# Splitting 32 of the 42 input projections of the second block into three f32r products each

## The reference, cut to what matters

```python
def second_block(x, norm_mix, w_in, sinks, lam_re, ...):
    h = rms_norm(x, norm_mix[l])
    qa, ka, va, u, qm, km, vm, gates = split_in(h @ w_in[l])
    oa = swa_attention(qa, ka, va, sinks[l], slopes_swa)
    ya = oa @ w_o_swa[l]
    ys = s5_ssm(u, ...)
    z = jax.nn.gelu(ys).astype(x.dtype) @ w_glu[l]
    yb = (z[..., :SSM_WIDTH] * jax.nn.sigmoid(z[..., SSM_WIDTH:])) @ w_o_ssm[l]
    om = moba_attention(qm, km, vm, slopes_moba)
    yc = om @ w_o_moba[l]
    g = jax.nn.sigmoid(gates)
    mixed = (g[..., :D_MODEL] * ya + g[..., D_MODEL:2 * D_MODEL] * yb
             + g[..., 2 * D_MODEL:] * yc)
    x = x + mixed @ w_out[l]
```

## Time and profile before

| | us |
|---|---|
| median of 3 runs | 2204.14 |
| lowest and highest | 2203.28, 2205.13 |
| the profiled execution, its own time | 2205.18 |
| its span in the trace | 2203.4 |
| PE busy, share of the span | 2121.9, 96% |
| DVE busy | 853.8, 39% |
| ACT busy | 543.4, 25% |
| POOL busy | 89.9, 4% |

### The profile page before, as it was taken

One profiled execution on the slowest core, in us unless ns is written; L12 is line 12 of the kernel. 1 busy time (PEld: TensorE's weight loads), 2 busy tenths in 40 slices (PEclk: granted clock), 3 DMA queues, 4 the chain that ended last, 5 costly groups with the idle time before them and its releaser, 6 DMA issues.

```text
span 2203.4 us, 35696 instructions
## 1 busy us (share of the span) xinstructions
PE 2121.9 (96%) x15114; PEld 1312.8 (60%) x15114; DVE 853.8 (39%) x1576; ACT 543.4 (25%) x1013; POOL 89.9 (4%) x109
## 2 busy tenths in 40 slices
PE   6999999999999999998889999999999999999998
PEld 2666688888864673433323343334433877889998
DVE  4798523334532432032001210110022467666765
ACT  4124322224431421011000100000011134444443
POOL 0000000000000000000000000000501200001300
PEclk9999999999999999999989999999999999999999
DMA  9885232323211549999999999999995332344451
GB/s 387 333 354 191 77 115 77 114 76 105 82 39 47 207 184 379 355 376 402 417 413 408 389 402 378 407 401 418 413 405 212 127 115 77 115 152 174 173 189 57
DMA packets 160740, 536.71 MB, mean 244 GB/s; under 512 B 7120, under 2 KB 31824, under 8 KB 139728
## 3 DMA queue, kind: packets, MB, share of 16 engines
q1 hardware_dynamic: 160448, 534.08, 63.4%
q0 software_dynamic: 144, 0.52, 0.1%
HBM read 533.53 MB, written 1.05 MB: 243 GB/s over the span
## 4 chain that ended last, share of the span: by engine, by line
PE 84%; DVE 6%; DMA 5%; DVEq 3%; issue 1%; ACT 1%; SPq 0%; ACTq 0%
PE psum L1422 15%; PE psum L968 11%; PE psum L975 10%; PE psum L976 10%; PE psum L977 10%; PE psum L1426 7%; PE psum L1447 7%; PE psum L1451 3%; DMA X<-in_o_exp_w 2%; DVE region L2344 2%; DVEq L2347 1%; PE psum L992 1%; DMA region<-in_o_exp_w 1%; PE psum L1349 1%; DMA ring<-in_o_exp_w 1%
## 5 line engine op out<-in xcount | busy, mean ns | idle before, releaser
L975 PE MATMUL psum<-region_r 128*128 128x512 f32 (+1 forms) x1360 | 468.2, 344 | 14.2 <-DVE region L2356 3.2
L976 PE MATMUL psum<-region_r 128*128 128x512 f32 (+1 forms) x1264 | 425.4, 337 | 0.0
L977 PE MATMUL psum<-region_r 128*128 128x512 f32 (+1 forms) x1136 | 388.0, 342 | 0.0
L975 PEld LDWEIGHTS psum<-region_r 128*128 128x128 f32 x1360 | 258.7, 190 | 59.6 <-issue 20.3
L976 PEld LDWEIGHTS psum<-region_r 128*128 128x128 f32 x1264 | 240.7, 190 | 24.6
L977 PEld LDWEIGHTS psum<-region_r 128*128 128x128 f32 x1136 | 215.5, 190 | 24.8
L1422 PE MATMUL psum<-ring,region 128*32 128x512 f32 (+1 forms) x2064 | 203.8, 527 | 0.8 <-DMA ring<-in_o_exp_w 0.8
L1422 PEld LDWEIGHTS psum<-ring,region 128*32 128x32 f32 x2064 | 65.9, 111 | 118.4 <-issue 102.7
L968 PE MATMUL psum<-H,ring 128*128 128x256 f32 x576 | 128.7, 380 | 0.0
L968 PEld LDWEIGHTS psum<-H,ring 128*128 128x128 f32 x576 | 108.3, 190 | 16.5 <-ACT region L2059 1.3
L1983 ACT ACTIVATE region<-psum 128x256 f32<-128x256 f32 (+2 forms) x56 | 24.8, 450 | 376.2 <-PE psum L1373 278.0
(11 more groups left out here) (399 smaller groups left out, 2679.2 us busy)
## 6 DMA issues: line engine op xcount, KB each, us to landing
ring<-in_o_exp_w SPq DMA_DIRECT2D x151, 1024.0 KB, 12.4
region<-in_o_exp_w SPq DMA_DIRECT2D x118, 1024.0 KB, 14.2
ring<-in_w_ada SPq DMA_DIRECT2D x24, 2048.0 KB, 10.1
H<-in_o_exp_w SPq DMA_DIRECT2D x46, 1024.0 KB, 15.0
ring<-in_w_ff SPq DMA_DIRECT2D x16, 2048.0 KB, 7.9
ring<-in_e_ffn_w SPq DMA_DIRECT2D x22, 1024.0 KB, 7.9
X<-in_o_exp_w SPq DMA_DIRECT2D x21, 1024.0 KB, 14.5
ring<-in_w_in SPq DMA_DIRECT2D x10, 2048.0 KB, 8.0
```

What stands on the lines that cost most here:

```text
L975: pe.matmul(out, a_hi, b_hi, start=first, stop=False)
L976: pe.matmul(out, a_hi, b_lo, start=False, stop=False)
L977: mm = pe.matmul(out, a_lo, b_hi, start=False, stop=last)
```

## The change

- The chunks are taken in the order A, QM, QA, B, gates. The ten items of A and QM stay whole and come first (`WHOLE` = 10 instead of nine). The 32 items of QA, B and the gates are of a new kind, "split", and fill the eight rounds with four each.
- A split item is `product` over eight tiles: 24 f32r products of 128x256 instead of eight float32 products.
- ACT rounds the weights of a split item (`proj_high`): two instructions of 128x512, or one of 128x1024, depending on the buffer. There are three such buffers, used in turn (the last four items use two). Three items are rounded ahead, before ACT copies `bb_T`; each later one right after the `take` of the item that had its buffer, which is mostly the one three before.
- POOL subtracts (`L3109`), from the ring's weights to the same place, in pieces of the same sizes: 21 or 22 items with two pieces of 128x512 and ten with one of 128x1024.
- The normed input is split once: ACT rounds it between the first eight `take`s, and DVE subtracts in place (eight instructions of 128x256) when the last whole item is done.
- The counts of the semaphores that this shares with other stages are raised to fit.

The diff, cut to its core:

```diff
-C2_A, C2_B, C2_QA, C2_QM, C2_GATE, C2_SWA, C2_GLU, C2_MOBA, C2_SSM, C2_OUT, C2_FF1, C2_FF2 = (
+C2_A, C2_QM, C2_QA, C2_B, C2_GATE, C2_SWA, C2_GLU, C2_MOBA, C2_SSM, C2_OUT, C2_FF1, C2_FF2 = (
     0, 1, 2, 3, 4, 10, 11, 12, 13, 14, 16, 24)
...
+        + [(C2_QA, "split", 128 * i, ("qa", i)) for i in range(4)]
+        + [(C2_B, "split", 0, ("u", 2)), (C2_B, "split", 128, ("u", 3)),
+           (C2_B, "split", 256, ("qm", 0)), (C2_B, "split", 384, ("qm", 1))]
+        + [(C2_GATE + i // 4, "split", 128 * (i % 4), ("gate", i)) for i in range(24)])
+WHOLE = sum(p[1] != "split" for p in PROJ)
+PROJ_UNITS = len(PROJ) - WHOLE
+UNIT_OF = [i % 3 for i in range(PROJ_UNITS - 4)] + [1, 0, 1, 0]
+UNITS_BEFORE = Z_GROUPS + PROJ_UNITS
+UNITS_AFTER = [[i for i in range(3, PROJ_UNITS) if max(j for j in range(i) if UNIT_OF[j] == UNIT_OF[i]) == after]
+               for after in range(PROJ_UNITS)]
...
+        proj_hi = reg_r(25600, KT, T)
+        proj_parts = [[(range(0, 4), rstd_r[:, 0, :]), (range(4, KT), rstd_r[:, 1, :])],
+                      [(range(0, 4), reg_r(16896, 512)), (range(4, KT), reg_r(27648, 512))],
+                      [(range(0, KT), reg_r(5120, 1024))]]
...
+                elif kind == "split":
+                    if t == WHOLE:
+                        pe.wait_ge(s_n_lo_ready, KT)
+                    pe.wait_ge(s_weights_lo, Z_GROUPS + t - WHOLE + 1)
+                    mm = product(b[:, 0:T], [(hi[:, k - ks[0], :], proj_unit(t, [k], ring_r)[:, 0, :], proj_hi[:, k, :], H_lo[:, 0, k, :])
+                                             for ks, hi in proj_pieces(t) for k in ks], True, True)
...
-            for t in CHUNK_ITEMS[C2_A] + CHUNK_ITEMS[C2_B]:
+            for t in range(WHOLE):
                 project(t)
...
+            def proj_high(t):
+                n = PROJ[t][0]
+                if t in (items[0] for items in CHUNK_ITEMS):
+                    act.wait_ge(w_in[n % RING], landed2(n))
+                for ks, hi in proj_pieces(t):
+                    a = act.activation(hi, proj_unit(t, ks), ACT.Copy)
+                a.then_inc(s_weights_hi, 1)
...
                 a.then_inc(s_proj_sb, 1)
+                if t >= WHOLE:
+                    for ahead in UNITS_AFTER[t - WHOLE]:
+                        proj_high(WHOLE + ahead)
...
+            for t in range(WHOLE):
                 take(t)
+                if t < KT:
+                    act.wait_ge(s_h_ready, h_before(N_MIX2) + t + 1)
+                    act.activation(proj_hi[:, t, :], H[:, 0, t, :], ACT.Copy).then_inc(s_tile_hi, 1)
+            act.wait_ge(s_diag_ready, 1)
+            for i in range(3):
+                proj_high(WHOLE + i)
...
+            dve.wait_ge(s_proj_ready, WHOLE)
+            for k in range(KT):
+                dve.wait_ge(s_tile_hi, 2 * KT + k + 1)
+                dve.tensor_tensor(H_lo[:, 0, k, :], H[:, 0, k, :], proj_hi[:, k, :].bitcast(F32), ALU.subtract).then_inc(s_n_lo_ready, 1)
...
+            for t in range(WHOLE, len(PROJ)):
+                pool.wait_ge(s_weights_hi, Z_GROUPS + t - WHOLE + 1)
+                for ks, hi in proj_pieces(t):
+                    x = pool.tensor_tensor(proj_unit(t, ks, ring_r), proj_unit(t, ks), hi.bitcast(F32), ALU.subtract)
+                x.then_inc(s_weights_lo, 1)
```

More of the change, by code:

```diff
@@ L249 @@
 BRANCH_UNITS = 4 * len(BRANCHES)
-UNITS_BEFORE, VALUES_BEFORE = Z_GROUPS, 4
+VALUES_BEFORE = 4
 B_SPLIT = 4
@@ L361 @@
 PROJ = ([(C2_A, "dup", 0, ("ka", 0)), (C2_A, "dup", 64, ("ka", 1)), (C2_A, "tok", 128, ("va", 0)),
-         (C2_A, "feat", 256, ("u", 0)), (C2_A, "feat", 384, ("u", 1)),
-         (C2_B, "feat", 0, ("u", 2)), (C2_B, "feat", 128, ("u", 3)),
-         (C2_B, "feat", 256, ("qm", 0)), (C2_B, "feat", 384, ("qm", 1))]
-        + [(C2_QA, "feat", 128 * i, ("qa", i)) for i in range(4)]
+         (C2_A, "feat", 256, ("u", 0)), (C2_A, "feat", 384, ("u", 1))]
         + [(C2_QM, "feat", 128 * i, ("qm", 2 + i)) for i in range(2)]
         + [(C2_QM, "dup", 256, ("km", 0)), (C2_QM, "dup", 320, ("km", 1)), (C2_QM, "tok", 384, ("vm", 0))]
-        + [(C2_GATE + i // 4, "feat", 128 * (i % 4), ("gate", i)) for i in range(24)])
+        + [(C2_QA, "split", 128 * i, ("qa", i)) for i in range(4)]
[8 more added lines that the diff above has]
+               for after in range(PROJ_UNITS)]
 CHUNK_ITEMS = [[t for t, p in enumerate(PROJ) if p[0] == c] for c in range(C2_SWA)]
@@ L572, in build @@
         gain = sb("gain", P, 4, KT, 2)
-        rstd = sb("rstd", P, 2, 512)
+        with nc.sbuf_tensor("rstd", [P, 2, 512], F32) as rstd:
+            pass
+        rstd_r = sb("rstd_r", P, 2, 512, dt=F32R)
         warm = sb("warm", P, 1)
@@ L784, in branch_hi, with proj_unit, proj_pieces @@
             return unit_hi[u % B_SPLIT].rearrange("p (k h c) -> p k h c", k=4, h=2)
+        proj_hi = reg_r(25600, KT, T)
+        proj_parts = [[(range(0, 4), rstd_r[:, 0, :]), (range(4, KT), rstd_r[:, 1, :])],
+                      [(range(0, 4), reg_r(16896, 512)), (range(4, KT), reg_r(27648, 512))],
+                      [(range(0, KT), reg_r(5120, 1024))]]
+        def proj_unit(t, ks, memory=ring):
+            n, _, c, _ = PROJ[t]
+            return memory[:, n % RING, :].rearrange("p (k n) -> p k n", k=KT)[:, ks[0]:ks[-1] + 1, c:c + P]
+        def proj_pieces(t):
+            return [(ks, v.rearrange("p (k n) -> p k n", n=P)) for ks, v in proj_parts[UNIT_OF[t - WHOLE]]]
         def cols(w, c, n, rows=None):
```

6 lines of the change are left out of this document (3 added, 3 removed).

## The result

The changed kernel takes 2252.8 us (median of 4 runs, 2250.8 to 2256.5) against 2204.6 for the kernel before beside it: 1.022 times as long, with a 95% interval of 1.0202 to 1.0237. The forecast was 2241 in a range of 2212 to 2264. The profiled execution of the changed kernel is its longest one (2256.5, span 2254.7); set against the profile of before (2203.4) it is 51.3 longer, 3 more than the medians say.

The account below looks back on a forecast made before the run. The prediction took PE and DVE as balanced, with DVE's chain bounding the rounds up to the first `turn2`. Its terms, -0.5 + 0.6 + 14 + 18 + 6 = +38, less 1 for rounding, on 2204.1 gave 2241 us, range 2212 to 2264.

Parts of the forecast that it names:

- Making PE faster there gains nothing: In the rounds, from the drive to the first `turn2`, the chain needs DVE alone for 12.4 us; PE's items fit beside.
- Rival 1: In the rounds PE is the bound after all and POOL's work hides, so the gain arrives: 2191 us; chance 5%.
- Rivals 2 and 3: DVE and POOL collide only in slack (2204 to 2208, 8%), or only in elementwise instructions, not scans (2219, 15%).
- Rival 4: In the rounds POOL becomes the bound at 4 us an item, giving rounds of 28: 2265 to 2300; chance 10%.
- Ahead of the rounds: Before round 0: one more whole item, +3.5, and ACT's rounding before the `bb_T` copies, +3.0; together +6.5 us.
- Rounds 0 and 1 and the later rounds without contention: Rounds 0 and 1 save 7 us; six later rounds lose 0.6 from ACT's rounding against faster items.
- The -4 behind the first `turn2` of round 1: Behind that `turn2`, one split item replaces two items, 2.85 against 6.9 us: -4.
- The -3 ahead of it: From the first `state_input` to the first `turn2`, 27 us of work where the trace has 30.0: -3.
- ACT's +1.0 a round: In later rounds, rounding the next item delays `take_turned` of the second head, for which `values` waits: +1.0 us each.
- Contention, predicted +14 and +18: POOL's subtractions block DVE instructions with two SBUF inputs: +14 us in rounds 0 and 1, +18 later with the tail.
- The clock, predicted +6: PE waits 4 to 5 us before the first `turn2`, then runs at about half speed: +6, between 0 and 10.
- -6.4: The rounds without contention: -7 us for rounds 0 and 1 and +0.6 for the later rounds.

Follow-up runs that it names:

- e4: The changed kernel without POOL's subtractions and without ACT's rounding of the weights, PE still running the three f32r products; 2206.7 us, 1.0007 of the kernel before.
- e8: e4 with all four items of a round ahead of the first `turn2`, and ACT's order changed to match; 2187.8 us, 0.992 of the kernel before.
- e1: The changed kernel with POOL subtracting nothing, PE's third product reading the rounded weights instead of the low parts; 2209.2 us, 1.0013 of the kernel before.
- e2: The changed kernel with each POOL subtraction replaced by two memsets of the same tile, which read nothing; 2209.3 us, 1.0016 of the kernel before.
- e11: e9 with `bb_T` copied first, later ACT rounding, and per round three items subtracted on DVE, one on POOL at set places; 2213.7 us.
- e5: The changed kernel with useless matmuls on PE in front of the first `turn2` of rounds 1 to 7; 2244.4 us, 1.0175 of the kernel before.
- e9: The changed kernel, whole computation, in e8's order, with a round's subtractions shared, two on POOL and two on DVE; 2224.6 us, 1.0082 of the kernel before.

## Why the prediction was right, and where its steps were off

**Right: which engine bounds.** "Making PE faster there gains nothing": e4 has 15.5 us less of PE and the same time as before (some 3 us by the medians do arrive behind the start of the rounds, and the tenth whole item takes them back). Rival 1 (2191) is refuted in this order of the work. e8 shows under which condition it would hold. The prediction charged the halved clock to a wait that was more than half contention (2.4 us of 4 to 5). e4 shows that a part of it needs no contention: 20.4 us at half clock with POOL idle, of the changed kernel's 61.3.

**Right: contention is the term that decides.** e1 and e2 show it: without POOL's reads 43.6 and 43.5 of the 48.1 us go. Rivals 2 and 3 are refuted by e1 and by the scan's own row (612 against 434 ns). Rival 4 is too: POOL's subtraction took 1.35 and 2.40 us, against the 1.27 and 2.35 I took from the earlier trace rows, and POOL waits for ACT most of the time. One thing was wrong in how the two take turns: I had POOL at up to 5 us an item beside DVE. Its longest subtractions are 1.53 us for 512 elements and 2.60 for 1024, so nearly all the waiting is on DVE's side.

**Ahead of the rounds, predicted +6.5, measured +6.8.** Both parts are there: +3.9 in e4 (one more whole item), +2.8 for ACT's rounding (e1 less e4). e11, which copies `bb_T` first, has only the 3.9, though its round 0 is 3.0 us longer (18.4 against 15.4).

**Rounds 0 and 1 and the later rounds without contention, predicted -7 and +0.6.** Mis-sized by some 3 us. By the medians of e1 the rounds and what follows are 3.3 - 6.8 = -3.5. The traces of seven rounds scatter about that: +0.7 in e1, whose profile is its longest execution, and -4.6 in e2, whose profile is its shortest. They show which step held. The -4 behind the first `turn2` of round 1 came when POOL does not read: 9.6 us before, 6.1 in e1, 6.3 in e4. The -3 ahead of it came nearly where the clock was whole in round 0, and not where it wasn't: 30.0 us before, 27.5 in e2 and 27.7 in e4, but 29.8 in e1, where the granted clock is 0.5 from 1751.8 to 1758.7. In rounds 2 to 6 e2 has +0.2, and e1 +4.4 with 10.2 us at half clock. So what I left out is that PE's clock falls without contention too; I had put it into the sum only together with contention. In the changed kernel the -4 shrank to -1.0 (8.6 us), with the clock at half from 1787.1 to 1804.2 and the items meant to be faster at 0.21 a product. ACT's +1.0 a round did not show (e1 against e4: 2.5 in all by the medians, no more than the 2.8 ahead of the rounds).

**Contention, predicted +14 and +18; with the clock +38.** Against e1, round 1 of the changed kernel is 16.2 us longer (36.6 against 20.4), the next five are 20.5 longer and the rest 4.5: 41.2, and 43.6 by the medians. Round 1 is as reckoned: 13.7 of its 16.2 lie ahead of the first `turn2` (28.0 against 14.3), where I had +14. The later rounds were under-sized: some 4 us each, with clock, and up to 6.3 in round 5, where I had 2.5 to 3 and the clock's 0.9. The step that failed is where a round's four subtractions fall. I let one fall harmlessly into the drive and `biased`, and two into the second scan. In round 3 one met `biased` after all, in a two-column `tensor_scalar` that I had not counted as a user of the shared interface (+1.0), one the first scan (+2.1), one the first addition of `normalised` (+2.1), and the second scan none. PE's wait for the first `turn2` was accordingly longer than the 4 to 5 us I had named, 5.6 on average in rounds 2 to 7. I had counted how much of DVE's work has two SBUF inputs, where it mattered that any such instruction, however small, waits until POOL's is through.

**The clock, predicted +6.** e5 gives back 8.4 by holding the clock for 44 of the 61 us. Inside the range of 0 to 10, and a little more than was taken.

**The sum.** +6.5 was +6.8; -6.4 was about -3.5 by the medians; +38 was +43.6: +38.1 against +46.9, of the 48.1 measured. All misses point the same way, and the forecast ended 12 us low.

What stays open: e8's 18.9 us were measured without ACT's rounding of the weights as well. No run has its order with the rounding and without the subtractions, so it is not shown how much of the gain the rounding leaves; in e9 and e11, PE waits 12.8 and 9.5 us for ACT's copies at `turn2`. Why e11's two engines at 132.9 and 131.7 us of work need 152.3 was not taken further. Splitting only the six plain items that the kernel before has ahead of the rounds, where PE alone is on the chain, was not tried: at 3.46 less 2.85 us each it could give at most 3.7 us, which this measurement hardly tells from nothing.
